# Two sums of down-projection weight quarters moved from adding transfers to VectorE

## The reference

```python
def conv_ffn(x, norm_g, w_up, conv_w, conv_b, w_down):
    h = rms_norm(x, norm_g)
    a, b = jnp.split(h @ w_up, 2, axis=-1)
    a = lax.conv_general_dilated(a, conv_w[:, None, :], ...) + conv_b
    return (jax.nn.silu(a) * b) @ w_down          # 512 x 2816 times 2816 x 1024
...
x = x + conv_ffn(x, ffn_norm[l], w_up[l], conv_w[l], conv_b[l], w_down[l])
```

## Time and profile before

| | |
|---|---|
| median of 3 runs | 1580.63 us |
| the profiled execution's own time | 1578.9 us |
| its span | 1577.1 us |
| TensorE busy | 1561.3 us (99%) |
| VectorE busy | 1171.0 us (74%) |
| ScalarE busy | 769.3 us (49%) |
| GpSimd busy | 251.2 us (16%) |
| down stage of layer 0, TensorE | 676.3 to 788.7 us |
| down stage of layer 1, TensorE | 1457.3 to 1571.2 us |

### The profile page before, as it was taken

How to read it: one execution, slowest core, us unless ns; L and a number is a source line. 1 busy time by engine, 2 the same in 40 slices (tenths; PEclk the granted TensorE clock), 3 DMA queues, 4 the chain that set the end, 5 groups by cost and what they waited for, 6 DMA issues and landing times.

```text
span 1577.1 us, 22764 instructions
## 1 busy us (share of the span) xinstructions
PE 1561.3 (99%) x9106; PEld 1376.8 (87%) x9106; DVE 1171.0 (74%) x1295; ACT 769.3 (49%) x982; POOL 251.2 (16%) x270
## 2 busy tenths in 40 slices
PE   9999999999999999999999999999999999999998
PEld 7888888888888999999988888888888889999776
DVE  7258876686679877796982678758856798878877
ACT  5344334642356555564633543355422566556646
POOL 4000000000130222242240000000002212223310
PEclk9999999999999999999999999999999999999999
DMA  5342222222227888899223322222222288888991
GB/s 195 96 121 78 81 81 94 75 74 93 94 94 240 232 237 239 255 246 260 103 94 97 117 81 80 81 94 68 80 95 94 94 249 239 240 241 276 233 274 57
DMA packets 66628, 231.41 MB, mean 147 GB/s; under 512 B 7392, under 2 KB 7904, under 8 KB 66528
## 3 DMA queue, kind: packets, MB, share of 16 engines
q1 hardware_dynamic: 52272, 182.93, 33.4%
q0 software_dynamic: 12096, 41.95, 14.6%
q10 hardware_dynamic: 2160, 5.12, 1.1%
HBM read 225.78 MB, written 2.10 MB: 144 GB/s over the span
## 4 chain that ended last, share of the span: by engine, by line
PE 89%; DVE 5%; DMA 3%; issue 2%; ACT 1%; POOL 0%; DVEq 0%; ACTq 0%; POOLq 0%
PE ps L1756 17%; PE ps L1757 17%; PE ps L1758 17%; PE ps L1762 11%; PE ps L1764 11%; PE ps L1763 11%; DMA far_raw<-wdn 2%; PE ps L1885 1%; PE ps L1874 1%; PE ps L1852 1%; PE ps L1856 1%; DMA w_raw<-wdn 1%; DVE comb_lo L1347 1%; PE ps L2009 0%; DVE w_lo L1194 0%
## 5 line engine op out<-in xcount | busy, mean ns | idle before, releaser
L1756 PE MATMUL ps<-u_hi,w_hi 128*128 128x512 f32 x768 | 301.3, 392 | 0.0
L1757 PE MATMUL ps<-u_lo,w_hi 128*128 128x512 f32 x768 | 299.3, 390 | 0.0
L1758 PE MATMUL ps<-u_hi,w_lo 128*128 128x512 f32 x768 | 299.1, 389 | 0.0
L1194 DVE TENSOR_TENSOR w_lo<-w_raw,w_hi 128x1024 fp32r<-128x1024 f32 x158 | 208.4, 1332 | 68.6 <-ACT w_hi L760 68.3
L760 ACT ACTIVATE w_hi<-w_raw 128x1024 fp32r<-128x1024 f32 x158 | 164.2, 1053 | 77.6 <-DMA w_raw<-wts 71.3
L1758 PEld LDWEIGHTS ps<-u_hi,w_lo 128*128 128x128 f32 x768 | 144.2, 188 | 30.4
L1756 PEld LDWEIGHTS ps<-u_hi,w_hi 128*128 128x128 f32 x768 | 144.3, 188 | 28.5
L1757 PEld LDWEIGHTS ps<-u_lo,w_hi 128*128 128x128 f32 x768 | 144.4, 188 | 28.2
L1762 PE MATMUL ps<-comb_hi,far_hi 128*128 128x256 f32 x576 | 161.3, 280 | 0.8 <-issue 0.7
L1763 PE MATMUL ps<-comb_lo,far_hi 128*128 128x256 f32 x576 | 160.7, 279 | 0.0
L1764 PE MATMUL ps<-comb_hi,far_lo 128*128 128x256 f32 x512 | 143.3, 280 | 0.0
(11 more groups left out here) (307 smaller groups left out, 3719.3 us busy)
## 6 DMA issues: line engine op xcount, KB each, us to landing
w_raw<-wts SPq DMA_DIRECT2D x212, 512.0 KB, 3.5
far_raw<-wts SPq DMA_DIRECT2D x56, 512.0 KB, 4.1
t_raw<-wdn POOLq DMA_DIRECT2D x30, 512.0 KB, 9.6
w_raw<-wdn SPq DMA_DIRECT2D x24, 512.0 KB, 7.1
w_raw<-wts POOLq DMA_DIRECT2D x18, 512.0 KB, 10.2
far_raw<-wts POOLq DMA_DIRECT2D x16, 512.0 KB, 7.1
far_raw<-wdn SPq DMA_DIRECT2D x16, 512.0 KB, 8.2
t_raw<-wdn SPq DMA_DIRECT2D x10, 512.0 KB, 5.4
```

The costliest lines, as they stand in the source:

```text
L1194: nc.vector.tensor_tensor(w_lo[:, s, :], w_raw[:, s, :], w_hi[:, s, :].bitcast(F32), ALU.subtract).then_inc(s_lo, 1)
L1756: nc.tensor.matmul(dst, a_hi, b_hi, start=start, stop=False)
L1757: nc.tensor.matmul(dst, a_hi, b_lo, start=False, stop=False)
L1758: return nc.tensor.matmul(dst, a_lo, b_hi, start=False, stop=stop)
```

## The change

1. Product 1's operand: `load_sum` loads W12 in place of W11 into `t_raw`, and VectorE adds the loaded piece of W11 (unit j's raw piece) to it (`second_weights`, six additions a layer). The six adding transfers of `first_sums` are gone.
2. Product 4's operand: VectorE adds the loaded piece of product 5 (W22) to that of product 4 (W12) (`fifth_weights`, six a layer, at the steps of `FIFTH_AT`). The six adding transfers at L711 are gone. The pieces of product 5 are therefore loaded earlier.
3. Two raw slots more (`SPARE`, `SPARE + 1`), which lie where the last two high slots lay; the high parts go through six slots after unit 7. `RAW_SLOT`, `HI_SLOT` and the order of loading are new.
4. The transposes of layer 1 use four banks (0, 1, 6, 7) in place of two.

```diff
+SPARE = FAR + 4
-RAW_SLOT = [RAW_ORDER + [FAR, FAR + 1], RAW_ORDER + [3, 1]]
-HI_ORDER = [(2, 1, 0, FAR, FAR + 1, FAR + 2, FAR + 3, 3)[u % 8] for u in range(UNITS_DOWN)]
+RAW_SLOT = [RAW_ORDER, RAW_ORDER]
+HI_ORDER = [(2, 1, 0, FAR, FAR + 1, FAR + 2, FAR + 3, 3)[u] if u < 8 else (FAR + 1, 3, 2, 1, 0, FAR)[u % 6] for u in range(UNITS_DOWN)]
+FIFTH_AT = {16: 0, 17: 1, 22: 2, 24: 3, 25: 4, 26: 5}
...
-                sp.dma_start(t_raw[:, j, 0:piece(j)], wdn[l * 4 + W11, :, j * 1024:j * 1024 + piece(j)]).then_inc(s_tland[int(j > 1)], 16)
+                sp.dma_start(t_raw[:, j, 0:piece(j)], wdn[l * 4 + W12, :, j * 1024:j * 1024 + piece(j)]).then_inc(s_tland[int(j > 1)], 16)
...
-                first_sums(l)
                 gated(l, SPLIT - 1)
                 further_sums(l)
...
+            def second_weights(l, j):
+                unit_landed(l, j)
+                dve.wait_ge(s_tland[int(j > 1)], l * (32 + 32 * (j > 1)) + 32 + 32 * (j > 1))
+                nc.vector.tensor_tensor(unit_raw(l, PIECES + j), unit_raw(l, PIECES + j), unit_raw(l, j), ALU.add).then_inc(s_sum4, 1)
+            def fifth_weights(l, j):
+                top, bottom = 4 * PIECES + j, 5 * PIECES + j
+                unit_landed(l, top)
+                unit_landed(l, bottom)
+                nc.vector.tensor_tensor(unit_raw(l, top), unit_raw(l, top), unit_raw(l, bottom), ALU.add).then_inc(s_sum4, 1)
...
                     else:
+                        second_weights(l, 0)
+                        second_weights(l, 1)
                         unit_low(l, 0)
                         unit_low(l, 1)
...
                         chunk_low(l, 1)
+                        second_weights(l, 2)
                         unit_low(l, 2)
                 for t in range(UNITS_DOWN):
                     if t % 6 == 1 and t > 6:
                         take_product(l, t // 6 - 1)
+                    if t in FIFTH_AT:
+                        fifth_weights(l, FIFTH_AT[t])
+                    if t + 3 < PIECES:
+                        second_weights(l, t + 3)
                     if t + 3 < UNITS_DOWN:
                         unit_low(l, t + 3)
...
-                    if g >= 2:
-                        pe.wait_ge(s_moved, g - 1)
+                    if g >= 4:
+                        pe.wait_ge(s_moved, g - 3)
```

More of the change, by code:

```diff
@@ L70, with vacated @@
 SUM_K = (1, 2, 4, 5)
+FIFTH_AT = {16: 0, 17: 1, 22: 2, 24: 3, 25: 4, 26: 5}
 def before(slots, u):
     return max((v for v in range(u) if slots[v] == slots[u]), default=None)
+def vacated(l, u):
+    if RAW_SLOT[l][u] >= SPARE and before(RAW_SLOT[l], u) is None:
+        return HI_SLOT[l].index(RAW_SLOT[l][u] - 2)
+    return before(RAW_SLOT[l], u)
 LOADED = [u for u in range(UNITS_DOWN) if u // PIECES in (0, 3, 4, 5)]
@@ L189, in trunk @@
         far_hi = sb("far_hi", [P, 4, SLAB], F32R, u_lo_at)
+        spare_at = u_lo_at + 2 * 4 * SLAB
+        spare_raw = sb("spare_raw", [P, 2, SLAB], F32, spare_at)
+        spare_lo = sb("spare_lo", [P, 2, SLAB], F32R, spare_at)
         w_hi_at = at[0]
@@ L290, in trunk @@
         s_fetch = [sem(f"s_fetch{k}") for k in range(KT)]
+        s_spare = sem("s_spare")
         s_par = sem("s_par")
@@ L495, in down_tile, with turn_bank @@
             return l * TILES + TILE_CREDIT + DOWN_TILE
+        def turn_bank(g):
+            return (0, 1, 6, 7)[g % 4]
         def token_rows(tt):
@@ L562, in load_unit @@
                 quarter = {0: W11, 3: W21, 4: W12, 5: W22}[k]
-                sp.dma_start(unit_raw(l, u), wdn[l * 4 + quarter, :, j * 1024:j * 1024 + piece(j)]).then_inc(s_fetch[RAW_SLOT[l][u]], 16)
+                landed = s_fetch[RAW_SLOT[l][u]] if RAW_SLOT[l][u] < SPARE else s_spare
+                sp.dma_start(unit_raw(l, u), wdn[l * 4 + quarter, :, j * 1024:j * 1024 + piece(j)]).then_inc(landed, 16)
             def load_sum(l, j):
-                sp.dma_start(t_raw[:, j, 0:piece(j)], wdn[l * 4 + W11, :, j * 1024:j * 1024 + piece(j)]).then_inc(s_tland[int(j > 1)], 16)
+                sp.dma_start(t_raw[:, j, 0:piece(j)], wdn[l * 4 + W12, :, j * 1024:j * 1024 + piece(j)]).then_inc(s_tland[int(j > 1)], 16)
             def load_down(l):
@@ L581, in load_down @@
                 load_unit(l, 5)
-                for u in sorted(LOADED[PIECES:], key=lambda u: before(RAW_SLOT[l], u)):
-                    sp.wait_ge(s_unit, l * UNITS_DOWN + before(RAW_SLOT[l], u) + 1)
+                for u in sorted(LOADED[PIECES:], key=lambda u: vacated(l, u)):
+                    sp.wait_ge(s_unit, l * UNITS_DOWN + vacated(l, u) + 1)
                     load_unit(l, u)
@@ L692, in add_piece @@
                                     accum_op=ALU.add).then_inc(s_tsum[j], 16)
-            def first_sums(l):
-                for j in range(PIECES):
-                    pool.wait_ge(s_tland[int(j > 1)], l * (32 + 32 * (j > 1)) + 32 + 32 * (j > 1))
-                    add_piece(l, j, W12)
             def further_sums(l):
@@ L705, in further_sums @@
                         add_piece(l, j, quarter)
-                for j in range(PIECES):
-                    u = 4 * PIECES + j
-                    s = RAW_SLOT[l][u]
-                    pool.wait_ge(s_tsum[j], l * 64 + 48)
-                    pool.wait_ge(s_fetch[s], 16 * (1 + l * arrivals_of_layer(u) + arrivals(u)))
-                    nc.gpsimd.dma_start(unit_raw(l, u), wdn[l * 4 + W22, :, j * 1024:j * 1024 + piece(j)],
-                                        accum_op=ALU.add).then_inc(s_tsum[j], 16)
             def gated(l, n):
@@ L825, in part_high @@
                 if k == 6:
-                    act.wait_ge(s_sum4, m + 1)
+                    act.wait_ge(s_sum4, l * (SPLIT + 2 * PIECES) + n + 1)
                     if n > 0:
@@ L860, in unit_high @@
                 k, j = divmod(u, PIECES)
-                if k in (1, 2, 6):
-                    act.wait_ge(s_tsum[j], l * 64 + {1: 16, 2: 32, 6: 48}[k])
-                elif k == 4:
-                    act.wait_ge(s_tsum[j], l * 64 + 64)
+                if k in (2, 6):
+                    act.wait_ge(s_tsum[j], l * 32 + {2: 16, 6: 32}[k])
+                elif k in (1, 4):
+                    act.wait_ge(s_sum4, l * (SPLIT + 2 * PIECES) + SPLIT + (PIECES if k == 4 else 0) + j + 1)
+                elif RAW_SLOT[l][u] >= SPARE:
+                    act.wait_ge(s_spare, 32 * (l + 1))
                 else:
@@ L2136, in _ @@
                 one(2, 2, False, False)
+                if l + 1 == DEPTH:
+                    pe.wait_ge(s_moved, 2 * TT)
                 one(3, 6, True, True)
```

19 lines of the change are left out of this document (12 added, 7 removed).

## The result

The changed kernel took **1595.12 us** (median of 6 runs, 1593.6 to 1596.6) where the kernel before took 1579.74 us (6 runs, 1578.29 to 1586.1): ratio 1.0088, 95% interval [1.0074, 1.0103]. It is slower by 14 to 15 us. The forecast was 1585 with a range of 1577 to 1590, so the time lies above the range.

A forecast was written before the change was run, and what follows sets the result against it. TensorE, busy 1561.3 of 1577.1 us, was taken as the bound, so only gaps could be won. Layer 0 5.0 + 1.0 - 2.9, layer 1 1.95 + 1.2 - 1.0: together +5.3 us, said as 1585, range 1577 to 1590.

The forecast's parts named there:

- Gaps of before that go: Down stages: TensorE's gaps of 2.9 us in layer 0, 1.0 and the bank's 1.4 in layer 1 vanish, 5.3 us.
- Entry, product 1: Start of each down stage: VectorE's six additions make TensorE 5.0 us late at unit 6, layer 0; +1.95 net in layer 1.
- Product 4: Units 24 to 28: VectorE's chain makes TensorE late, 1.0 us of 0 to 2.7 (layer 0), 1.2 of 0 to 3.4 (layer 1).
- Rival 2: Units 6 to 20: remaining adding transfers still fill the engines, the 2.9 and 1.0 us gaps stay; +8, 1587 us; chance 0.10.
- DMA share clearly below 1 after unit 20: Sign expected in the changed profile: behind unit 20 the DMA engines are no longer full.
- The prediction's own sign of being wrong: Wrong if entry waits sum below 3 us a layer, a transfer-ended gap stays, or product 4 and 5 gaps exceed 3 us.
- 56 us without a gap: Layer 0, 668.72 to 725.44 us: VectorE said to have no idle time, with six additions put into it.
- Rival 3: Product 4: VectorE idles for ScalarE three times with nothing spare, pieces 28 and 29 load late; 1588 to 1594 us; chance 0.14.
- Additions beside GpSimd: VectorE operations falling into GpSimd's multiplication: loss of 2.25 us charged once, as before, with no further loss.
- rival 4: Entry of each layer: two more additions each lose 2.07 us beside GpSimd's multiplications; +8 on the forecast, 1592 us; chance 0.05.
- Six high slots: High parts wait for the unit six before, VectorE is three to four ahead: no cost.

The follow-up runs named there:

- W21 later: Changed kernel with the adding transfers of W21 (product 6) held back to unit 24 + j: 1592.17 us, ratio 1.0080.
- TensorE kept at work: Changed kernel with 3.1 us of matmuls into a bank nobody reads, at the end of unit 27: 1592.07 us, ratio 1.0081.
- the read-out experiment: Changed kernel with product 4's additions for pieces 2 to 5 one step earlier, plus L1746 ahead of the second addition and unit 1's low part: 1587.76 us.

## Why the prediction was wrong

The experiments give each term of the sum its own price. In shares of the kernel before:

| | product 1 by transfers | product 1 by VectorE |
|---|---|---|
| product 4's additions late (as changed) | 1.0030 | 1.0088 |
| product 4's additions early | 0.9978 | 1.0050 |

and 0.9958 with no additions at all, 1.0032 with the late ones of product 4 alone and nothing for product 1.

- **Gaps of before that go:** forecast -5.3 us (2.9, 1.0 and the bank's 1.4). Found -6.6 us (0.9958 of 1579.7), in a kernel that has neither the twelve transfers nor an addition in their place. The size is right. Which of the two groups of transfers it comes from is not shown; taking away product 1's was worth nothing beside late additions, and the banks by themselves gave nothing that shows.
- **Entry, product 1:** forecast 5.0 us in layer 0 and 1.95 + 1.44 in layer 1, 8.4 together when set against a kernel without the bank wait. Found 0.0058 and 0.0072 of 1579.7 in the two rows of the table: 9.2 and 11.4 us, each good to some 3 us. Nearly right. The waits at unit 0 were forecast at 1.9 and are 1.90 and 1.90. Those at unit 4 were forecast at 2.6 and 1.4 and are 1.08 and 1.34: in layer 0 the slow clock behind unit 0 took up the rest (3.4 us at half pace, 1.7 us). Counted from the beginning of the stage, unit 6 starts 5.1 us later than before, as the sum had it. In the two other kernels with this entry in which the clock did not fall at unit 0 (W21 later; TensorE kept at work), unit 4 waits 2.65 and 2.69 us, as forecast, and in the first of them unit 6 is 5.0 us late all the same: the slow clock at the entry cost nothing there, since VectorE sets the place of unit 6. That VectorE's order is of no matter and its amount is, as the sum had it, the read-out experiment shows.
- **Product 4, the step that failed.** Forecast 1.0 + 1.2 us. Found 0.0074 of 1579.7, 11.7 us, between the kernel with these additions alone and the one with none. By the changed kernel's own rows: waits of 0.95, 0.33 and 3.44 us in layer 0 and 0.36 and 3.41 in layer 1, 8.5 us (the 0.95 is at unit 22, still product 3, where I had forecast none). The slow clock at unit 28 lies outside the waits for 3.4 and 5.35 us and so costs at most 4.4 us; the filling won 1.1 to 3.1 of it. Two things failed:
  - *The wait for the transfers of units 21 and 22, which I put at nothing.* I let VectorE wait for unit 20's piece alone and then run thirteen operations without a gap: 16.3 us from its low part to step 24. It took 748.67 - 728.95 = 19.7, with 2.51 and 0.63 us of idle time for the next two pieces. The kernel before idles 1.65 and 1.52 us at the same two units, so its own trace spoke against the sum; and where these waits were taken away (W21 later, changed kernel) it took 16.6 beside one short wait. The start I had at 730.4 at worst, and it was 728.95; the two additional waits were nowhere in the range. In layer 1 they are 1.44 and 0.40 us, and the wait of 3.41 us at unit 28 lies just at the end of the 0 to 3.4 forecast; I had taken 1.2. The low part for unit 28 ended at 758.5, where I had 752.7 or 756.4. Steps 24 and 25 were forecast at 9.7 us with idle times of 1.1 and took 757.65 + 0.87 - 748.67 = 9.85: the chain itself was right.
  - *The clock.* I took 0.118 us a matmul for fixed, from two windows in both of which TensorE was never idle. Before has no wait above 1.74 us in these stages, and in its profiled execution none of them is followed by a fall; nothing in its trace could show what a wait of 3.4 us does.
- **Rival 2, the transfers stay the bound,** had the cause of the late pieces, with a chance of 0.10. The share is 1.07 at 712 us, as before, though the share from 682 to 688 is 0.00 for 1.07: the transfers of product 1 taken away left a hole at the entry, and those of product 4 one behind 736 us, and neither lies where the pieces of units 20 to 22 were awaited. "DMA share clearly below 1 after unit 20" came true only from 736 us on.
- **The prediction's own sign of being wrong:** gaps of over 3 us a layer in products 4 and 5. They are 3.77 us in each layer (units 27 and 28).
- **A reading of the earlier trace rows:** "56 us without a gap" from 668.72 to 725.44 has the idle time of 7.20 us in it; without a gap were 49.5 us. The sum of the entry does not hang on it.
- **Rival 3, product 4's chain decides,** is what happened, at 1588 to 1594 with a chance of 0.14. I had its cause at pieces 28 and 29; it was at 21 and 22. The measured 1595 is above even its range. I took a price near the low end because of "a queue that is now lighter", which holds for the stage as a whole and not for this stretch of it.
- **Additions beside GpSimd:** no further loss. L1403 took 1.91 us for 0.75 and a low part 2.33 for 1.22, 2.3 us together, as before. In layer 1 one of the two that lost is an addition (2.35 for 1.22), and the loss is the same 2.2 us in all. So rival 4, 1592, has nothing for it. The Trainium skill (SBUF — State Buffer, "Who interferes with whom") states that whoever issues first gets the shared ports for the whole instruction, there for VectorE's two-port modes. The prediction took the trace to speak against this, since an operation lost 1.1 us of a multiplication's 2.07. That reading does not stand: in layer 0 of the changed kernel the two multiplications lie apart and are recorded with 1.31 and 1.56 us, so the 2.07 can hold waiting of GpSimd's own, and 1.1 us may be nearly a whole multiplication. Spans on GpSimd are rough, and no run settles it.
- **Six high slots:** as forecast, no cost. The longest wait of a high part for TensorE is 3.18 us, in product 6, as before (3.18), and TensorE has no wait there. In the waits of TensorE no line stands for a transfer.

Taken one after the other, -6.6, 11.7 and 9.2 us lead to 14.3 us; they are differences of the same runs, so this is no test of its own. What is left: between the two down stages the changed kernel takes 1.5 us more than before when the entry wait of layer 1 is set aside, of which the waits in the up parts explain 0.2, and ahead of the first down stage it takes 1.1 us less; the rest stays open.

## What to carry to other kernels

Work moved from transfers to an engine is paid where that engine has no gap, and frees the queue only where the transfers were: check in windows that the hole is made where the queue is full, and let the whole chain of pieces wait for its transfers, not the first one alone; the idle times of the kernel before at each piece are in its trace. An addition that feeds another engine's copy goes a step ahead of the user of that copy (6 to 8 us here, for a table of six numbers). And a wait of TensorE that grows past those the trace has shown without a fall of the clock is priced at more than its length.
